# Routing from the unnormalised x, overflow code ahead of the experts, and the last stage begun in the experts' tail

## The reference

```
h = _rmsnorm(x, norm_ffn[l])                       # x * rsqrt(mean(x*x) + eps) * gain
logits = xt @ router                               # xt: the 256 rows of h, router: 1024 x 8
top_logit, top_idx = lax.top_k(logits, 2)
gates = jax.nn.softmax(top_logit, axis=-1)
y = (silu(xt[token] @ w1[e]) * (xt[token] @ w3[e])) @ w2[e]    # per token and chosen expert, width 1408
x = x + sum over the two chosen experts of gate * y
x = second_block(x, norm_gain_2, w_in_2, ...)      # begins with h = rms_norm(x, norm_gain) and h @ w_in
```

## Time and profile before

| | |
|---|---|
| time, median of 3 runs (lowest to highest) | 1711.96 us (1711.75 to 1712.21) |
| time of the profiled run | 1712.29 us |
| its span | 1710.3 us, 24960 instructions |
| PE busy | 1582.5 us, 93% |
| DVE busy | 1135.5 us, 66% |
| ACT busy | 824.2 us, 48% |
| POOL busy | 11.0 us, 1% |
| HBM read | 290.22 MB, 170 GB/s over the span |

### The profile page before, as it was taken

One profiled execution on the slowest core, in us unless ns is written; L12 is line 12 of the kernel. 1 busy time (PEld: TensorE's weight loads), 2 busy tenths in 40 slices (PEclk: granted clock), 3 DMA queues, 4 the chain that ended last, 5 costly groups with the idle time before them and its releaser, 6 DMA issues. The chain is left out here.

```text
span 1710.3 us, 24960 instructions
## 1 busy us (share of the span) xinstructions
PE 1582.5 (93%) x10076; PEld 1374.7 (80%) x10076; DVE 1135.5 (66%) x1640; ACT 824.2 (48%) x1087; POOL 11.0 (1%) x12
## 2 busy tenths in 40 slices
PE   7989989989999898998997899999999969988998
PEld 6788979879999878898987767777777749976677
DVE  6699564655555669956465698888888845256634
ACT  4643335344444464333533576777777734344322
POOL 1000000000000000000000000000000000000000
PEclk9999999999999899999998799999999978789999
DMA  7432222335555343222233199999999954412221
GB/s 283 141 112 88 85 99 87 112 136 185 186 188 191 131 136 112 87 87 99 87 111 123 50 344 346 339 343 340 342 367 336 340 170 160 148 62 75 75 73 75
DMA packets 82053, 292.98 MB, mean 171 GB/s; under 512 B 9095, under 2 KB 11647, under 8 KB 81679
## 3 DMA queue, kind: packets, MB, share of 16 engines
q1 hardware_dynamic: 81791, 290.10, 48.6%
q10 hardware_dynamic: 144, 1.24, 0.2%
HBM read 290.22 MB, written 1.08 MB: 170 GB/s over the span
## 5 line engine op out<-in xcount | busy, mean ns | idle before, releaser
L360 DVE TENSOR_TENSOR ring_lo<-ring,weights_hi 128x1024 fp32r<-128x1024 f32 x359 | 433.1, 1222 | 263.8 <-ACT weights_hi L340 261.2
L267 PE MATMUL bank_P<-h_hi,weights_hi 128*128 128x256 f32 x1584 | 475.8, 300 | 38.6 <-DVE h_lo L1058 18.9
L340 ACT ACTIVATE weights_hi<-ring 128x1024 fp32r<-128x1024 f32 x359 | 371.9, 1055 | 224.1 <-PE bank_P L269 187.1
L269 PE MATMUL bank_P<-h_hi,ring_lo 128*128 128x256 f32 x1584 | 459.1, 290 | 0.0
L268 PE MATMUL bank_P<-h_lo,weights_hi 128*128 128x256 f32 x1584 | 458.6, 290 | 0.0
L267 PEld LDWEIGHTS bank_P<-h_hi,weights_hi 128*128 128x128 f32 x1584 | 312.4, 197 | 55.4 <-issue 26.8
L269 PEld LDWEIGHTS bank_P<-h_hi,ring_lo 128*128 128x128 f32 x1584 | 316.9, 200 | 0.0
L268 PEld LDWEIGHTS bank_P<-h_lo,weights_hi 128*128 128x128 f32 x1584 | 313.2, 198 | 1.7 <-issue 1.0
L268 PE MATMUL bank_P<-ring_lo,gathered_hi 128*96 128x512 f32 (+1 forms) x384 | 143.9, 375 | 0.0
L360 DVE TENSOR_TENSOR ring_lo<-ring,tokens_hi 128x1024 fp32r<-128x1024 f32 x76 | 90.4, 1216 | 2.3 <-ACT tokens_hi L340 2.3
L360 DVE TENSOR_TENSOR ring_lo<-ring,tokens_lo 128x1024 fp32r<-128x1024 f32 x74 | 88.2, 1217 | 2.3 <-ACT tokens_lo L340 2.3
(11 more groups left out here) (458 smaller groups left out, 2622.2 us busy)
## 6 DMA issues: line engine op xcount, KB each, us to landing
ring<-stream SPq DMA_DIRECT2D x541, 512.0 KB, 4.4
cst<-consts SPq DMA_DIRECT2D x1, 1712.0 KB, 10.3
arena<-params ACTq DMA_DIRECT2D x1, 1211.0 KB, 7.5
arena<-x SPq DMA_DIRECT2D x1, 1024.0 KB, 5.1
arena<-bias_vec SPq DMA_DIRECT2D x8, 128.0 KB
out<-arena SPq DMA_DIRECT2D x2, 512.0 KB
arena<-params SPq DMA_DIRECT2D x2, 256.0 KB, 7.1
arena<-bias_vec SPq DMA_DIRECT2D x8, 64.0 KB
```

Source lines behind the costliest of these rows:

```text
L267: pe.matmul(out, hi, x_hi, start=start, stop=False, skip_group_check=True)
L269: return pe.matmul(out, lo, x_hi, start=False, stop=stop, skip_group_check=True)
L340: a.activation(self.slots[i % len(self.slots)], env["ring"][:, slot, :], ACT.Copy)\
L360: v.tensor_tensor(env["ring_lo"][:, slot, :], env["ring"][:, slot, :], self.slots[i % len(self.slots)].bitcast(F32), ALU.subtract).then_in ...
```

## The change

`gathered_section` becomes two parts, a routing part that stays in the first block of sections, and the experts, which stand behind the overflow branch in one block with the last stage. So the branch is taken between routing and experts.

- Layer 1's mixer returns behind `x_3`. The gain is multiplied into the router beforehand (`router_gain`). The logits are made from x, 8 rows of 256 tokens in 8 products of 256 columns, and turned. x itself is turned into token rows by 16 transposes.
- ScalarE takes the sum of squares of each token from those rows (`accum_out`), then the square root; VectorE the reciprocal (`token_rms`). It scales the difference of the two logits and the token rows as they are split into `htm`. The channel gain is applied when the gathered tokens are copied out, and high and low parts are gathered into one bank, eight banks in turn.
- `params2` is loaded behind mix1's blocks, and the bias vector is made and stored during routing. GpSimd makes x times gain for the overflow code (`xg`), in 8 operations.
- `all_engine_barrier()` ahead of the branch goes; the one at the end of the block of sections stays.
- The high and low parts of the last stage's first two blocks are made at the end of the experts, VectorE's ahead of the addition to x; the squares wait for each `x_i`.
- The overflow code reads `xg`, scales by `token_rms`, and has a ring of 3 slots.

```
+    routing, experts = gathered_sections(env)
     run_sections(env, load=load_section(env), mix0=mix_section(env, 0), dense=dense_section(env),
-                 mix1=mix_section(env, 1), moe=gathered_section(env))
-    nc.all_engine_barrier()
+                 mix1=mix_section(env, 1), routing=routing)
     n_parts = nc.values_load(parts[0:1, :], min_val=0, max_val=EXPERTS)
     with nc.If(n_parts > 0):
         run_sections(env, overflow=overflow_section(env))
         nc.all_engine_barrier()
-    run_sections(env, second=second_section(env))
+    run_sections(env, moe=experts, second=second_section(env))
...
+        if layer:
+            env["mix1_blocks"] = blocks
+            return
...
+        if layer:
+            hi.upto(68)
+            return
...
+            tt(env["router_gain"], R("router", 0, 64).rearrange("p (k e) -> p k e", k=KD),
+               R("norm_ffn", 0, 8).unsqueeze(2).broadcast_to([P, KD, EXPERTS]), MUL, "router_gain")
...
+    def routing_sync(sp):
+        sp.wait_ge(*after("x_3", "dense"))
+        sp.dma_start(prm2, env["dram"]["params2"]).then_inc(env["sem"]("params2_in"), 16)
+        load_blocks(env, sp, MOE_AT, MOE_AT + RING)
+        sp.wait_ge(*after("vec"))
+        sp.wait_ge(*after("vec_end"))
+        sp.dma_start(env["dram"]["bias_vec"].rearrange("(i h) n -> h i n", i=2), vec[0:8, :, 0:512])\
+          .then_inc(env["sem"]("vec_stored"), 16)
+        sp.wait_ge(*after("parts"))
+
+    def routing_gpsimd(g):
+        g.wait_ge(*after("x_3", "mix1"))
+        for k in range(KD):
+            g.tensor_scalar(xg[:, k, :], x[:, k, :], gain(k), None, ALU.mult).then_inc(*done("pool", f"xg_{k}"))
+        g.memset(vec[0:8, :, VEC:VEC + 1], 0.0).then_inc(*done("pool", "vec_end"))
+        g.wait_ge(*after("parts"))
...
+        def logits(q):
+            for k in (2 * q, 2 * q + 1):
+                mm = pe.matmul(Z1[0:8, 0:T], rg[:, k, :], x[:, k, :], start=(k == 0), stop=(k == KD - 1))
+                if k == 0:
+                    env["mix1_blocks"].release(mm)
+            if q == 3:
+                mm.then_inc(*done("pe", "logitsT"))
+
+        def turn(q):
+            for k in (2 * q, 2 * q + 1):
+                for a in range(TT2):
+                    mm = pe.transpose(tm_bank(a, k // 4)[:, (k % 4) * P:(k % 4 + 1) * P], x[:, k, a * P:(a + 1) * P], ident)
+            if q % 2:
+                mm.then_inc(*done("pe", f"p_xT_{q // 2}"))
+
+        pe.wait_ge(*after("router_gain", "mix1"))
+        for q in range(4):
+            pe.wait_ge(*after(f"x_{q}", "mix1"))
+            logits(q)
+            turn(q)
+        pe.wait_ge(*after("lgT"))
         for a in range(TT2):
+            mm = pe.transpose(Z1[:, T + a * 8:T + a * 8 + 8], lgT[0:8, a * P:(a + 1) * P], ident[0:8, 0:8])
         mm.then_inc(*done("pe", "logits"))
+
+        pe.wait_ge(env["sem"]("params2_in"), 16)
+        for i in range(2):
+            mm = pe.matmul((P0, P1)[i][0:8, 0:VEC], R2("rel", 0, 8)[0:BUCKETS + 1, :],
+                           R2("onehot", i * VEC, VEC)[0:BUCKETS + 1, :], start=True, stop=True)
+        mm.then_inc(*done("pe", "p_vec"))
...
+    def routing_scalar(a):
+        for half in range(2):
+            a.wait_ge(*after(f"p_xT_{half}"))
+            for t in range(TT2):
+                a.activation(squares, tm_bank(t, half), ACT.Square, accum_out=ss[:, half, t:t + 1])\
+                 .then_inc(*done("act", f"squares_{half}_{t}"))
+                a.wait_ge(*after(f"squares_{half}_{t}"))
+        a.wait_ge(*after("token_squares"))
+        a.activation(rt, ss[:, 0, :], ACT.Sqrt, scale=1.0 / D, bias=eps("norm")).then_inc(*done("act", "token_root"))
+        a.wait_ge(*after("token_rms"))
+        for half in range(2):
+            for t in range(TT2):
+                a.activation(htm[0][:, t, half * 512:(half + 1) * 512], tm_bank(t, half), ACT.Identity, scale=rt[:, t:t + 1])\
+                 .then_inc(*done("act", f"htm_hi_{half}_{t}"))
+        a.wait_ge(*after("p_vec"))
+        for i in range(2):
+            a.activation(vec[0:8, i, 0:VEC], (P0, P1)[i][0:8, 0:VEC], ACT.Copy).then_inc(*done("act", "vec" if i else None))
+        a.wait_ge(*after("gate_diff"))
+        a.activation(dm, dm, ACT.Exp).then_inc(*done("act", "gate_exp"))
+        a.wait_ge(*after("parts"))
...
+            if not second:
+                v.wait_ge(*after("squares_1_1"))
+                tt(ss[:, 0, :], ss[:, 0, :], ss[:, 1, :], ADD, "token_squares")
+        tt(chosen, oh1, oh2, ADD, "chosen")
+        v.wait_ge(*after("token_root"))
+        link(v.reciprocal(rt, rt), "token_rms")
+        tt(dm, m2[:, :, 0], m1[:, :, 0], SUB)
+        tt(dm, dm, rt, MUL, "gate_diff")

+        def low_parts(half):
+            for t in range(TT2):
+                v.wait_ge(*after(f"htm_hi_{half}_{t}"))
+                c = slice(half * 512, (half + 1) * 512)
+                stt(htm[1][:, t, c], tm_bank(t, half), rt[:, t:t + 1], htm[0][:, t, c].bitcast(F32), MUL, SUB, f"htm_lo_{half}_{t}")
+
+        low_parts(0)
+        v.wait_ge(*after("ranks"))
+
...
+        ts(most[:, 1:2], most[:, 0:1], CAP + 0.5, float(EXPERTS), ALU.is_gt, MUL)
+        link(v.tensor_copy(parts, most[:, 1:2]), "parts")
+        slot_numbers = C("iota").unsqueeze(1).broadcast_to([P, EXPERTS, CAP])
+        for a in range(TT2):
+            tt(sel[:, :, a, :], slot_numbers, rank[:, a, :].unsqueeze(2).broadcast_to([P, EXPERTS, CAP]), ALU.is_equal,
+               "sel" if a else None)
+        low_parts(1)
+        v.wait_ge(*after("gate_exp"))
...
+        stt(wt, rank, CAP - 0.5, w8, ALU.is_gt, MUL, "weights")
...
+    def sync(sp):
+        load_blocks(env, sp, MOE_AT + RING, SEC_AT + RING)
+
+    def tensor(pe):
+        pe.wait_ge(*after("htm_lo_1_1", "routing"))
         for n in range(2 * KD):
             g, k = n // KD, n % KD
-            if n >= 4:
-                pe.wait_ge(*after(f"hE_hi_{n - 4}"))
-                pe.wait_ge(*after(f"hE_lo_{n - 4}"))
-            for part, bank in ((0, (P0, P1, Z0, Z1)[n % 4]), (1, (BO, BC, BY, BX)[n % 4])):
+            if n >= 8:
+                pe.wait_ge(*after(f"hE_lo_{n - 8}"))
+            for part in range(2):
                 for a in range(TT2):
-                    mm = pe.matmul(bank[:, 0:QUAD * CAP], htm[part][:, a, k * P:(k + 1) * P],
-                                   sel[:, g * QUAD:(g + 1) * QUAD, a, :], start=(a == 0), stop=(a == TT2 - 1))
-                mm.then_inc(*done("pe", f"p_hE_{('hi', 'lo')[part]}_{n}"))
+                    mm = pe.matmul(gather_banks[n % 8][:, 0:QUAD * CAP], htm[part][:, a, k * P:(k + 1) * P],
+                                   sel[:, g * QUAD:(g + 1) * QUAD, a, :], start=(part + a == 0), stop=(part + a == 2))
+            mm.then_inc(*done("pe", f"p_hE_{n}"))
...
-        a.activation(unit, ident, ACT.Copy).then_inc(*done("act", "unit"))
-        for i in range(8):
-            part, tok, half = i // 4, i // 2 % 2, i % 2
-            a.wait_ge(*after(f"p_htm_{i}"))
-            a.activation(htm[part][:, tok, half * 512:(half + 1) * 512], (BO, BC, BY, BX, P0, P1)[i % 6], ACT.Copy)\
-             .then_inc(*done("act", f"htm_{i}"))
-        a.wait_ge(*after("gate_diff"))
-        a.activation(dm, dm, ACT.Exp).then_inc(*done("act", "gate_exp"))
-        hi.upto(3)
+        hi.upto(2)
         for n in range(2 * KD):
             g, k = n // KD, n % KD
-            a.wait_ge(*after(f"p_hE_hi_{n}"))
+            if n == 12:
+                hi.upto(3)
+            a.wait_ge(*after(f"p_hE_{n}"))
             a.activation(hE[0][:, g * QUAD:(g + 1) * QUAD, k, :],
-                         (P0, P1, Z0, Z1)[n % 4][:, 0:QUAD * CAP].rearrange("p (e s) -> p e s", e=QUAD), ACT.Copy)\
+                         gather_banks[n % 8][:, 0:QUAD * CAP].rearrange("p (e s) -> p e s", e=QUAD), ACT.Identity, scale=gain(k))\
              .then_inc(*done("act", f"hE_hi_{n}"))
-        a.wait_ge(*after("p_hE_lo_15"))
...
+        env["second_hi_parts"] = HiParts(env, a, SEC_AT, SEC_SPLIT, "second")
+        env["second_hi_parts"].upto(2)
...
+        lo.upto(1)
         for n in range(2 * KD):
             g, k = n // KD, n % KD
-            if n == 8:
-                lo.upto(1)
-            v.wait_ge(*after(f"p_hE_lo_{n}"))
-            v.tensor_copy(hE[1][:, g * QUAD:(g + 1) * QUAD, k, :],
-                          (BO, BC, BY, BX)[n % 4][:, 0:QUAD * CAP].rearrange("p (e s) -> p e s", e=QUAD))\
+            if n == 12:
+                lo.upto(2)
+            v.wait_ge(*after(f"hE_hi_{n}"))
+            v.scalar_tensor_tensor(out=hE[1][:, g * QUAD:(g + 1) * QUAD, k, :],
+                                   in0=gather_banks[n % 8][:, 0:QUAD * CAP].rearrange("p (e s) -> p e s", e=QUAD), scalar=gain(k),
+                                   in1=hE[0][:, g * QUAD:(g + 1) * QUAD, k, :].bitcast(F32), op0=MUL, op1=SUB)\
              .then_inc(*done("dve", f"hE_lo_{n}"))
...
+        env["second_lo_parts"] = LoParts(env, v, SEC_AT, SEC_SPLIT, "second")
```

(56 more changed lines are left out.)

139 lines of the change are left out of this document (70 added, 69 removed).

## The result

The changed kernel took 1683.12 us (median of 4 runs, 1682.00 to 1684.62), the kernel before 1711.86 us (4 runs, 1711.23 to 1712.21) on the same chip: a ratio of 0.9833, 95% interval 0.9816 to 0.9850. I had forecast 1682, so the time is 1.1 us off. The profiled run took 1684.62 us, with a span of 1682.8 against 1710.3 before: 27.5 us less. The total hides two errors of opposite sign, so I take the 27.5 us apart by places that both programs have.

What follows compares the result with a forecast made beforehand. PE was taken to pace the experts, with little DMA room, so gains come only from the edges: 12.1 + 3.8 + 14.5 = 30.4 us off 1712.29 gives 1681.9, adjusted to the median and rounded to 1682; range 1675 to 1693.

Steps and rivals of the forecast that it cites:

- The first edge: Routing and gather, up to the first expert product: it would come at 956.1 instead of 968.18, a gain of 12.1 us.
- VectorE alone sets the time, 940.4.: End of routing: after the ranks, VectorE's small operations, selection and low parts alone set the pace, ending at 940.4.
- Barrier, load of the number and branch ... With one I take 1.3 (bounds 0.8 and 1.57).: Between routing and gather: one barrier, number load and branch take 1.3 us, so the gather starts at 941.7, previously 954.20.
- Gather to first expert product, 14.4 us.: Gather from 941.7: 13.1 us of instructions, then ScalarE's copy and VectorE's low part; first expert product at 956.1.
- the rival with the larger gain: Shorter PE pauses keep full clock, so gather and the last stage's first tile are each 1.7 us shorter: 1678; chance 0.09.
- Experts, 3.8 us.: First expert: PE's wait for the fourth block's low part and the half clock behind it go, gaining 3.8 us.
- The DMA did not become the bound.: Rival in the experts: DMA becomes the bound and 15.9 us are given back: 1697; chance 0.06, including other waits that size.
- Last stage, 14.5 us.: Last edge: the root of the last stage's norm comes at 1384.6 instead of 1399.11, 14.5 us earlier.
- GpSimd, 0.65 us each, hidden.: Routing: GpSimd's eight scalings take 0.65 us each and stay under cover of the other engines' 17 us.
- The rival in which it keeps the barrier shut: End of routing: GpSimd's scalings, beyond 2.1 us each, delay the barrier; at 7 us each 1720; chance 0.02 for slower.
- From the root on nothing changes.: Last stage behind the root: 8.7 us to the first product and the rest stay as before, gain 0.
- That the search would be held up by 1 to 3 us: Routing: the search's two-input operations wait for GpSimd, 1.1 to 3.3 us later, 1683 to 1685, within the range.

Runs made afterwards that it cites:

- e9_params_late: The change with one more load of params2, issued from ScalarE's queue when x is complete, TensorE waiting for it before the last stage's ones product: 1697.36 us.
- e10_barrier_back: The change with its last section in a block of its own, so a barrier of all engines stands between x complete and the squares: 1687.60 us.
- e7_no_xg: The change without GpSimd's eight scalings of x for the overflow code: 1682.84 us.
- e2: The change without overflow code, number load, branch, or barrier between routing and experts (one block, with one added wait): 1683.44 us.
- e6: The change with selection, exponential and gate weights behind the branch, and VectorE's two last-stage low parts behind the additions to x: 1679.00 us.
- e3_short_pe: The change with TensorE's overflow loop taken out; barrier, number load, branch and the other engines' overflow code stay: 1680.54 us.
- e1_no_branch: The change without the overflow code, the load of its number and the branch; the barrier at the block's end stays: 1679.49 us.

## Why the prediction was right

**Right in total, and partly by luck.** Two of the three places sized from rows held to 0.4 us. The first edge was put 5.1 us too high, and 0.6 us were lost ahead of it; against that stand 2.4 us behind the root and 0.4 us at the last edge that I had not counted. The 2.4 us hang on how the clock fell, to which the change has no sure claim (see below); that they came is luck. By the profiled run, which the sum was made for, I was 2.7 us off (1681.9 against 1684.62); that run was the slowest of the four, and so the median lies only 1.1 us from 1682.

- *VectorE alone sets the time, 940.4.* Right. Its last operation ends 18.95 us after TensorE's start, 18.2 forecast. The logits, transposes, search and ranks came within 0.6 us of their steps, the first two low parts within 0.9, and the bias vector's products were at full clock and covered.
- *"Barrier, load of the number and branch ... With one I take 1.3 (bounds 0.8 and 1.57)."* This is the step that failed. The row it came from showed a DMA issued by ScalarE, that is, ScalarE's price, and for ScalarE it holds: 1.23 us. TensorE's is 4.58, beyond my upper bound: 0.55 for the barrier, 0.87 for load and branch, 3.16 for its own long jump. Before the change TensorE jumped under the 7.49 us load of params2 and nobody waited for it: the packet of q8 moved between 1383 and 1384 us there, 2.8 us behind x, and TensorE's first product waited until 1389.35 for the load. I had asked what the removed branch was worth at the last edge, and not what cover it had there.
- *Gather to first expert product, 14.4 us.* 15.45. I had two supplies within 0.6 us of each other and took the wrong one: VectorE's low parts take 0.61, not 0.56, a low part of the weights (1.22) stands ahead of the last four, and they end 1.7 us behind TensorE's last product. The clock, too, was at its half level (granted 0.50) up to 951, so the gather's first 4.7 us ran at half, where it was 3.4 before; the rival with the larger gain did not come about.
- *Experts, 3.8 us.* Right: no wait for the fourth block's low part, clock 1.00. One wait for a low part stays in the first expert, 0.74 us at 984.38, but it was there before as well (0.76). The DMA did not become the bound.
- *Last stage, 14.5 us.* 14.9. x was complete 5.74 us after y (6.2 forecast), and the ones product was at full clock. e9_params_late and e10_barrier_back show both causes: the load with its half clock is 11.45 us of it, and a barrier 2.1, by holding the squares until the whole of x is there. The remaining 1.3 us were not taken apart.
- *GpSimd, 0.65 us each, hidden.* 0.90 each, done at 930.98, hidden. The rival in which it keeps the barrier shut would have needed 2.1.
- *From the root on nothing changes.* 2.4 us less, and not by the work, which is the same. See below. I had also called 1407.84 the stage's first product; it was at 1404.40, 5.3 us after the root, and after the change it is 5.2 us after it. The sum doesn't use it.

**Where the 2.4 us are.** Rows of PE by stretch, from 20 to 30 us behind the root, with granted clock in the third column from the end; first of the kernel before, then of the change, then of e7_no_xg, whose last stage is that of the change to the letter:

```profile
1419.11:1429.11 10.00, 8.02 (x55) 7.81 (x55) 6.01 (x9) 3.34 (x4) 0.00 (x0) 0.83 0.36 129
```

```profile
1394.02:1404.02 10.00, 8.32 (x70) 8.32 (x71) 5.20 (x7) 5.38 (x7) 0.00 (x0) 1.00 0.42 136
```

```profile
1390.40:1400.40 10.00, 8.02 (x55) 7.82 (x55) 6.05 (x9) 3.34 (x4) 0.00 (x0) 0.83 0.37 122
```

A short pause of TensorE lies there, and in some profiles the clock falls to its half level behind it and in others not. Where it falls (before, e2, e6, e7, e9), root to end is 310.8 to 312.8 us; where it doesn't (the other nine), 308.5 to 309.6. The two groups differ earlier as well. TensorE waits 5 us between the norm's ones product and the first product behind the root, every profile is at half level over 5 to 10 us behind the root, and in the five that fall later the clock is slower to come back: the granted clock over 10 to 15 us is 0.64 to 0.75 in them and 0.82 to 0.98 in the nine. Since e7 falls with the change's own code, the change has no sure claim to the 2.4 us. Before its root the kernel before had a long wait, as e9 has; why e7, e2 and e6 come back late is not shown.

## What to carry to other kernels

Price a branch for each engine by itself: the engine with long code to jump over pays most, and the place to branch is where that engine waits for something else anyway, or the long code should be kept out of the way. A price read from a row belongs to the engine and the cover of that row. Where runs spread by as much as an edit is worth, measure from place to place inside the profiles, and look at the granted clock before crediting the rest to the edit.

## What was unexpected of the hardware

- A jump of TensorE over its whole overflow loop costs about 3 us more than one over 33 of the loop's 239 products, transposes and releases, and over twice the loop at most 0.6 more than over one. With it goes a packet of an "instruction" queue, 2.4 to 2.6 us ahead of TensorE's next product in nine profiles. The Trainium skill, Advanced Engine Details and Errata, Control Flow Timing, gives about 108 ns for a compare-and-branch: by that the branch would be nearly free. ScalarE's 1.23 us and TensorE's 1.42 us over no loop, both with barrier and load, don't contradict it; TensorE's 4.58 us is far beyond it.
- The clock ahead of any edit: the copy stands between 925.17 and 930.70 us in the thirteen profiles of the table, whose work up to there is the same (but for GpSimd's in e7_no_xg). Over the first 100 us the granted clock was 0.91 in e3_short_pe (copy at 930.70) and 0.95 in e1_no_branch (925.60):

```profile
0.00:100.00 100.00, 83.53 (x535) 74.09 (x535) 67.52 (x101) 49.40 (x62) 7.28 (x8) 0.91 0.57 202
```

```profile
0.00:100.00 100.00, 83.81 (x552) 74.73 (x553) 69.48 (x108) 51.44 (x65) 7.28 (x8) 0.95 0.57 204
```

- GpSimd reading x beside VectorE's search held up one conversion by 0.24 us and no other step. The Trainium skill, SBUF — State Buffer, Who interferes with whom, names a cast among the instructions that can exclude GpSimd, and two-input instructions, of which none ran while the scalings did (923.76 to 930.98; the next one started at 931.04): the trace agrees. That the search would be held up by 1 to 3 us, as I had weighed it, did not come about, since the scalings were over by its first half.
